# Down projections of a three-block forward pass: moving tiles read as two interleaved halves of the tokens

## What is computed

```python
def swiglu(h, w_gate, w_up, w_down):
    return (jax.nn.silu(h @ w_gate) * (h @ w_up)) @ w_down

x = x + swiglu(rmsnorm(x, g), w_gate, w_up, w_down)   # w_down: 2816 x 1024, three times
```

## Time and profile before

| | |
|---|---|
| median of 3 runs | 1705.97 us (1705.41 to 1706.67) |
| the profiled execution | 1705.69 us, of which its span is 1703.9 us |
| mean granted TensorE clock | 0.996 of full |
| TensorE busy | 1679.6 us of the span |
| VectorE, ScalarE, GpSimd busy | 1262.3, 854.9 and 528.4 us |

### The profile page before, as it was taken

The page is one execution under the profiler, slowest core; times in us unless marked ns, Lnnn a source line. Parts: engine busy times, 40 slices in busy tenths (PEclk is TensorE's granted clock), DMA queues, the critical chain, the costliest instruction groups (busy, mean ns, idle before and its releaser), DMA issues.

```text
span 1703.9 us, 27591 instructions
## 1 busy us (share of the span) xinstructions
PE 1679.6 (99%) x10716; PEld 1457.6 (86%) x10716; DVE 1262.3 (74%) x1752; ACT 854.9 (50%) x1314; POOL 528.4 (31%) x368
## 2 busy tenths in 40 slices
PE   9989999999999999999999999999999999999997
PEld 7867789988998866789988998788888998899886
DVE  7767789845876798788845886688858885488575
ACT  6448367724763322557723764433335673277342
POOL 1451125503530446325503540121402560255000
PEclk9999999999999999999999999999999999999999
DMA  6310224333433565223433342422222333333332
GB/s 223 89 50 2 87 70 116 95 112 93 121 100 103 125 154 142 79 75 100 119 108 97 100 117 85 130 75 75 78 72 74 100 102 110 112 100 98 113 93 80
DMA packets 284923, 169.11 MB, mean 99 GB/s; under 512 B 8336, under 2 KB 278880, under 8 KB 284800
## 3 DMA queue, kind: packets, MB, share of 16 engines
q1 hardware_dynamic: 283792, 165.16, 34.5%
q0 software_dynamic: 720, 1.72, 0.3%
q10 hardware_dynamic: 288, 0.54, 0.1%
HBM read 156.71 MB, written 2.10 MB: 93 GB/s over the span
## 4 chain that ended last, share of the span: by engine, by line
PE 50%; DVE 4%; ACT 1%; issue 1%; DVEq 0%; ACTq 0%
PE ps L1443 21%; PE ps L1093 9%; PE ps L1095 9%; PE ps L1094 9%; DVE w L1792 1%; PE ps L1657 1%; ACT w L629 1%; DVE w L2120 1%; ACT w L799 0%; DVE act_lo L1824 0%; DVE bt_lo L1822 0%; DVE rstd L1834 0%; DVE tt L2136 0%; DVE x L2622 0%; PE ps L1670 0%
## 5 line engine op out<-in xcount | busy, mean ns | idle before, releaser
L1093 PE MATMUL ps<-act_hi,w 128*128 128x512 f32 x788 | 313.3, 398 | 5.3 <-DVE act_lo L1824 1.5
L1095 PE MATMUL ps<-act_hi,w 128*128 128x512 f32 x788 | 307.8, 391 | 0.0
L1094 PE MATMUL ps<-act_lo,w 128*128 128x512 f32 x788 | 307.6, 390 | 0.0
L1443 PE MATMUL ps<-act_hi,w 128*128 128x256 f32 (+1 forms) x1461 | 270.3, 277 | 1.7 <-DVE w L2120 1.2
L629 ACT ACTIVATE w<-raw 128x2048 fp32r<-128x2048 f32 (+2 forms) x102 | 163.6, 1604 | 200.1 <-PE ps L1095 186.3
L1443 PEld LDWEIGHTS ps<-act_hi,w 128*128 128x128 f32 x1461 | 229.4, 188 | 3.7 <-DVE w L2120 1.8
L1792 DVE TENSOR_TENSOR w<-raw,w 128x2048 fp32r<-128x2048 f32 (+2 forms) x93 | 181.3, 1950 | 41.0 <-ACT w L629 40.7
L466 POOL TENSOR_TENSOR raw<-raw 128x512 f32<-128x512 f32 x60 | 81.5, 1359 | 412.1 <-DVE sqacc L1812 165.6
L1093 PE MATMUL ps<-hid_hi,w 128*128 128x512 f32 x528 | 205.5, 389 | 0.0
L1094 PE MATMUL ps<-hid_lo,w 128*128 128x512 f32 x528 | 205.5, 389 | 0.0
L1095 PE MATMUL ps<-hid_hi,w 128*128 128x512 f32 x528 | 205.4, 389 | 0.0
(11 more groups left out here) (430 smaller groups left out, 3590.9 us busy)
## 6 DMA issues: line engine op xcount, KB each, us to landing
raw<-in_ffn_w_gate_dram SPq DMA_DIRECT2D x44, 512.0 KB, 4.0
raw<-in_ffn_w_up_dram SPq DMA_DIRECT2D x44, 512.0 KB, 5.2
raw<-in_w_gate_upffn_dram SPq DMA_DIRECT2D x44, 512.0 KB, 4.5
raw<-in_ffn_w_down_dram SPq DMA_DIRECT2D x32, 384.0 KB, 4.2
raw<-in_conv_w_pw_dram SPq DMA_DIRECT2D x24, 512.0 KB, 5.6
raw<-in_w_in_dram SPq DMA_DIRECT2D x24, 512.0 KB, 4.4
raw<-in_ffn_w_down_dram SPq DMA_DIRECT2D x32, 320.0 KB, 3.7
z<-z SPq DMA_DIRECT2D x30, 262.0 KB, 4.9
```

Source lines behind the costliest of these rows:

```text
L1093: pe.matmul(out, lhs[0], rhs[0], start=start, stop=False)
L1094: pe.matmul(out, lhs[0], rhs[1], start=False, stop=False)
L1095: return pe.matmul(out, lhs[1], rhs[0], start=False, stop=stop)
L1443: ins = pe.matmul(out[:, c], lhs, rhs[:, k, c], start=start and k == 0 and rhs is b_hi and lhs is w_hi, stop=k == Q4 - 1 and lhs is w_lo, ...
```

## The change

In the three down projections each moving tile is read in another order: token 0, token 256, token 1, token 257, and so on. The access pattern has an inner dimension of 2 elements that lie 256 elements (1024 bytes) apart, and an outer one of 256 neighbouring elements. The number of matmuls and of columns is the same, and the tiles in SBUF are written as before. A bank then holds token c at column 2c and token 256 + c at column 2c + 1. VectorE's multiplication by `rstd` puts the tokens back in order: it reads the bank with a step of two, first the even and then the odd columns, and writes `t2` in the usual order. The addition to `x` is as before.

```diff
+        def halves(v):
+            return v.rearrange("p (h c) -> p c h", h=2)
+
+        def by_half(v):
+            return v.rearrange("p (h c) -> p h c", h=2)
+
+        def in_turn(b):
+            return b[:, :].rearrange("p (c h) -> p h c", h=2)
...
-                        tile(T0[dn] + m, 0, lambda k: slot(nd, k, P), lambda k: (hid_hi[:, k], hid_lo[:, k]),
+                        tile(T0[dn] + m, 0, lambda k: slot(nd, k, P), lambda k: (halves(hid_hi[:, k]), halves(hid_lo[:, k])),
...
-                        seq.link(ve.tensor_tensor(t2[:, m % 2], bank(T0[dn] + m)[:, :], rstd[:, :], ALU.mult))
+                        seq.link(ve.tensor_tensor(by_half(t2[:, m % 2]), in_turn(bank(T0[dn] + m)), by_half(rstd[:, :]),
+                                                  ALU.mult))
```

## The result

The changed kernel takes 1688.99 us (median of 4 runs, 1687.26 to 1689.91) against 1705.69 us for the kernel before in the same comparison (1704.21 to 1706.67, 4 runs). The ratio is 0.9902, with a 95% interval of 0.989 to 0.9915. The profiled execution took 1688.09 us, of which 1686.3 us are its span; the prediction was 1688.2 us.

What follows compares the result with a forecast made beforehand. TensorE's matmul count times start distance was taken to bound the down projections. 1494 x 11.7 ns = 17.5 us off the profiled 1705.69 us gave 1688.2 us; likeliest case 1685 to 1691 us, 8 in 10 range 1684 to 2030 us.

Steps and rivals of the forecast that it cites:

- half of plain float32's 430: Down projections: plain float32 matmuls of 512 columns start 430 ns apart; half, 215 ns, was forecast in place of 226.7.
- If they come from following one run at full rate, they go: TensorE's moving reads: two runs in turn, each read at half rate, free the clocks, giving 215 ns; chance of faster 0.43.
- the lost clocks: Down projections: fp32r takes 544 clocks for 512 columns, 32 over one a column, one lost in 16 columns.
- the order is not felt: Rival: TensorE's down projections stay at 226.7 ns, only VectorE's read counts; 1705.7 to 1707.3 us, chance 0.17.
- a fetch of each column: Rival: TensorE's moving read in all 1584 matmuls costs 430 ns or more, near 2026 us or 2707 us; chance 0.33.
- far price of 860 ns: TensorE's moving read: each column's fetch costs double plain float32's pace, 2707 us; chance 0.14.
- A price at each jump back: Rival: each of 256 inner-dimension ends in a down matmul costs one clock, 107 ns a matmul, 1873 us; chance 0.07.
- The count of 1494 matmuls: Of 1584 down matmuls, 3 x 30 at the part ends gain nothing, since TensorE waits there; 1494 x 11.7 ns = 17.5 us.
- VectorE's read: 48 instructions of 692 ns reading PSUM with a step of two; extra cost taken as zero, at most 0.53 us each.
- The 1.6 us at the part ends: Upper bound for VectorE's slower bank read where it is on the path, three part ends: 3 x 0.53 us.

Runs made afterwards that it cites:

- VectorE's part alone: Against the kernel before: TensorE reads in order, only VectorE reads the bank with a step of two, so tokens come out in another order; 1704.48 us, ratio 0.9997.

## Why the prediction was right

**The distance.** 215 ns was forecast from half of plain float32's 430, and 215.8 was measured. The six clocks over 512 that are left are close to the eight over 1024 that the plain stream has.

**The mechanism behind it was not right.** The step that failed is "If they come from following one run at full rate, they go". It fits the outcome, but two places in turn at 8 bytes keep the lost clocks (226.7 ns), and four runs in turn, each at a quarter of the rate, take 283 ns. Half the rate per run happened to give the right number. Any other reason that frees nearly all of the 32 lost clocks would have given it as well, so that part of the hit is luck. The reason in its place is only partly settled (below).

**The rivals.** That the order is not felt is out: 226.7 would have stayed. A price near the one named for a fetch of each column (433 and 451 against 430 ns) exists, but only for the two orders with a plain step; orders that return to their places cost between 216 and 340 ns. I gave this rival 0.33 and had no row to exclude it. Its far price of 860 ns appeared nowhere. A price at each jump back is out as well: the kernel has 256 of them in a matmul and is at 518 clocks.

**Where the gain is lost.** The count of 1494 matmuls held: the first matmul of tile 7 in part b is still 7.09 us ahead of the next stage's first (7.10 before). 1494 x (226.67 - 215.83) = 16.2 us. The trace has a little more: from the first matmul of a down projection to the first one of the stage behind it, the six take 369.3 us before and 352.6 us after, 16.7 us less. A small term was left out, some 0.3 us: behind the 256-column matmuls the first twelve matmuls of each of the six stages are slower than the pace of the stage, if the tiles are read in order. The starts of the first and the sixth matmul, before and then after:

```profile
345.93 0.40 PE L1093 MATMUL ps<-hid_hi,w 128*128 128x512 f32 x1
...
347.09 0.39 PE L1095 MATMUL ps<-hid_hi,w 128*128 128x512 f32 x1
```

```profile
344.72 0.38 PE L1104 MATMUL ps<-hid_hi,w 128*128 128x512 f32 x1
...
345.80 0.38 PE L1106 MATMUL ps<-hid_hi,w 128*128 128x512 f32 x1
```

That is 1.16 / 5 = 232 ns where the pace is 226.7, and 1.08 / 5 = 216 ns, the plain pace. What slows these first matmuls is not shown. The semaphore that TensorE checks there for each k does not explain it: the same tile checks it for every later k too, at 226.7 ns.

**The rest of the difference.** The profiled execution lies at 1688.09 us, within 0.1 us of the forecast, and that closeness is luck. Of the 17.6 us between the spans 16.7 are gained in the six stages, where 17.5 were forecast, mostly because the distance came out at 215.8 and not 215 ns. The other 0.9 us lie where nothing was changed. The first down projection starts at 344.72 us in place of 345.93 already, and nearly all of that comes from one stretch, from 273 to 298 us, here before and then after:

```profile
273.00:298.00 25.00, 25.00 (x215) 25.00 (x214) 22.72 (x29) 17.26 (x30) 14.46 (x11) 1.00 0.45 124
...
273.00:298.00 25.00, 25.00 (x222) 25.00 (x222) 22.94 (x31) 17.50 (x31) 14.32 (x10) 1.00 0.47 127
```

In the profiled execution of the kernel before, the 256-column matmuls of the up projection start 117.8 ns apart there, and in that of the changed kernel 113.3 ns, at the same full clock. The kernel with VectorE's part alone, which reads in order, has 113.3 ns there as well, so this is not the change. The changed kernel has such stretches later instead, and 0.9 us remain in sum. What makes such stretches is not shown. The medians differ by 16.7 us, which is what the six stages give.

**VectorE's read.** Taken at zero between 0 and 0.53 us: 691 ns. The 1.6 us at the part ends did not come.

## What to carry to other kernels

A fp32r matmul of 512 columns that is bound by its own stream took 227 ns in this kernel if the moving operand was read in order and 216 ns if two runs 16, 64 or 1024 bytes apart were read column by column in turn, and the readers of the bank undid it at no measurable cost with a step of two. The other orders tried gave nothing or lost: 8 bytes apart changed nothing, a step of two cost double, pairs 50% more. At 256 columns only 1.6 ns were gained, probably because a weight load for each matmul comes next.

## What the runs showed of the hardware

Clocks of the 2.4 GHz level for 512 columns, from the distances above (the mean granted clock was 0.995 to 0.998 of full in all of these profiles):

```
in order 0 1 2 3                          544
two in turn, 8 bytes apart (0 2 1 3)      544
two in turn, 16, 64 or 1024 bytes apart   518
halves in turn, four at a time            600
four runs in turn                         680
halves in turn, two at a time             816
each column 64 bytes on                  1040
step of two                              1083
```

One way of counting fits five of these eight lines. Take every second column alone and count how many of its columns in a row lie in the same 16 bytes: four with two runs 16 bytes or more apart (518 clocks), two in order and at 8 bytes apart (544), one with a step of 64 bytes or of two (1040 and 1083, whose difference it leaves open). The other three lines speak against it as it stands: four at a time counts two like the order in memory and is at 600, and four runs in turn and pairs count one and are at 680 and 816. That even and odd columns are fetched apart would be the mechanism to such a count; it is an assumption that no run tests.

The Trainium skill, SBUF — State Buffer, Specifications (TRN2), gives lines of 16 bytes and asks for two accesses to a line for full bandwidth. The step from 8 to 16 bytes agrees with the size of the line, and the doubling at 64 bytes on with the price of leaving it each time. Three measurements differ from the rule, and they decide: the order 0 1 2 3, with four accesses to a line, loses 26 clocks; a step of two, with two accesses to a line, costs double; and the fastest order changes the line with every column. Which property of the order in memory costs the lost clocks stays open.

VectorE reads PSUM with a step of 2 in 691 ns and with a step of 32 elements in 692 ns, where it took 692 in order, and ScalarE with a step of 2 in 376 ns, where it took 375.
